# Delta rule: the third inverse level issues all its first steps, two projection triples, then all its second steps, instead of alternating them

## The reference

```
a_mat = jnp.where(strict, jnp.einsum('bhnid,bhnjd->bhnij', kb, k) * decay, 0.0)
ia = a_mat + jnp.eye(c, dtype=a_mat.dtype)
u = lax.linalg.triangular_solve(ia, vb, left_side=True, lower=True, unit_diagonal=True)
w = lax.linalg.triangular_solve(ia, kb * jnp.exp(g)[..., None], left_side=True, lower=True,
                                unit_diagonal=True)
...
def step(s, xs):
    q_c, k_c, u_c, w_c, qk_c, sd_c = xs
    v_new = u_c - jnp.einsum('bhck,bhkv->bhcv', w_c, s)
    o_c = jnp.einsum('bhck,bhkv->bhcv', q_c, s) + jnp.einsum('bhij,bhjv->bhiv', qk_c, v_new)
    s = s * sd_c[..., None, None] + jnp.einsum('bhck,bhcv->bhkv', k_c, v_new)
    return s, o_c
```

## Time and profile before

| | us |
|---|---|
| median of 3 runs | 1801.79 |
| lowest, highest | 1801.58, 1805.0 |
| the profiled execution, its own time | 1799.56 |
| its span | 1797.8 |
| PE busy in the span | 1774.6 |
| DVE busy | 990.5 |
| ACT busy | 720.6 |

### The profile page before, as it was taken

How to read it: one execution, slowest core, us unless ns; L and a number is a source line. 1 busy time by engine, 2 the same in 40 slices (tenths; PEclk the granted TensorE clock), 3 DMA queues, 4 the chain that set the end, 5 groups by cost and what they waited for, 6 DMA issues and landing times.

```text
span 1797.8 us, 26545 instructions
## 1 busy us (share of the span) xinstructions
PE 1774.6 (99%) x10559; PEld 1438.3 (80%) x10559; DVE 990.5 (55%) x1669; ACT 720.6 (40%) x1382; POOL 126.5 (7%) x105
## 2 busy tenths in 40 slices
PE   8999999999999999999999999999999999999999
PEld 6788888888887888888888788468877778888887
DVE  4645656467537444444444755744423688777434
ACT  5644656456345211111134623755223532222324
POOL 1113031221001000000000001520000000000000
PEclk9999999999999999999999999999999999999999
DMA  6422222222324333333223451013313222233221
GB/s 194 85 61 71 61 72 55 56 72 68 109 94 116 107 93 93 98 102 103 94 94 95 91 118 48 24 50 115 118 55 110 71 94 93 93 98 111 95 76 65
DMA packets 183183, 158.18 MB, mean 88 GB/s; under 512 B 36977, under 2 KB 179886, under 8 KB 183050
## 3 DMA queue, kind: packets, MB, share of 16 engines
q1 hardware_dynamic: 172672, 152.88, 27.9%
q0 software_dynamic: 1248, 3.19, 1.3%
q10 hardware_dynamic: 9163, 0.72, 0.4%
HBM read 152.77 MB, written 3.73 MB: 87 GB/s over the span
## 4 chain that ended last, share of the span: by engine, by line
PE 90%; DVE 4%; ACT 3%; issue 1%; DMA 1%; ACTq 0%; POOL 0%; DVEq 0%
PE bank L744 13%; PE bank L746 13%; PE bank L745 13%; PE bank L845 5%; PE bank L847 5%; PE bank L846 5%; PE bank L945 4%; PE bank L734 4%; PE bank L947 4%; PE bank L946 4%; PE bank L1072 1%; PE bank L1083 1%; PE bank L1136 1%; PE bank L1335 1%; PE bank L1094 1%
## 5 line engine op out<-in xcount | busy, mean ns | idle before, releaser
L1539 ACT ACTIVATE w_hi<-ring 128x2048 fp32r<-128x2048 f32 x122 | 234.0, 1918 | 534.2 <-PE bank L746 375.7
L744 PE MATMUL bank<-h_hi,w_hi 128*128 128x512 f32 x1024 | 400.5, 391 | 2.2 <-DVE w_lo L2162 2.0
L746 PE MATMUL bank<-h_hi,w_lo 128*128 128x512 f32 x1024 | 398.5, 389 | 0.0
L745 PE MATMUL bank<-h_lo,w_hi 128*128 128x512 f32 x1024 | 398.4, 389 | 0.0
L2162 DVE TENSOR_TENSOR w_lo<-ring,w_hi 128x2048 fp32r<-128x2048 f32 x108 | 247.3, 2289 | 256.6 <-ACT w_hi L1539 256.6
L744 PEld LDWEIGHTS bank<-h_hi,w_hi 128*128 128x128 f32 x1024 | 192.2, 188 | 44.9 <-issue 3.6
L745 PEld LDWEIGHTS bank<-h_lo,w_hi 128*128 128x128 f32 x1024 | 192.3, 188 | 40.2 <-issue 0.5
L746 PEld LDWEIGHTS bank<-h_hi,w_lo 128*128 128x128 f32 x1024 | 192.3, 188 | 39.8
L845 PE MATMUL bank<-h_hi,w_hi 128*128 128x512 f32 x432 | 170.3, 394 | 1.7 <-DVE arena L2851 1.0
L847 PE MATMUL bank<-h_hi,w_lo 128*128 128x512 f32 x432 | 168.3, 390 | 0.0
L846 PE MATMUL bank<-h_lo,w_hi 128*128 128x512 f32 x432 | 168.1, 389 | 0.0
(11 more groups left out here) (449 smaller groups left out, 2496.5 us busy)
## 6 DMA issues: line engine op xcount, KB each, us to landing
ring<-in_sc_w_in SPq DMA_DIRECT2D x32, 1024.0 KB, 5.4
ring<-in_gdn_w_in SPq DMA_DIRECT2D x24, 1024.0 KB, 5.4
ring<-in_w_up SPq DMA_DIRECT2D x22, 1024.0 KB, 5.1
ring<-in_gdn_w_out SPq DMA_DIRECT2D x8, 1024.0 KB, 5.2
ring<-in_sc_w_out SPq DMA_DIRECT2D x8, 1024.0 KB, 5.2
ring<-in_w_down SPq DMA_DIRECT2D x8, 1024.0 KB, 5.2
ring<-in_w_in SPq DMA_DIRECT2D x4, 1024.0 KB, 5.6
ring<-in_w_mk SPq DMA_DIRECT2D x4, 1024.0 KB, 5.2
```

What stands on the lines that cost most here:

```text
L744: pe.matmul(o, a_hi(k), b_hi(k), start=(k == tiles[0]), stop=False)
L745: pe.matmul(o, a_hi(k), b_lo(k), start=False, stop=False)
L746: mm = pe.matmul(o, a_lo(k), b_hi(k), start=False, stop=(k == tiles[-1]))
L1539: act.activation(w_hi[:, plan[n]["pair"], :], ring[:, n % 2, :], ACT.Copy).then_inc(w_hi_ready, 1)
```

## The change

In the third level (`lv` = 2) the kernel before issues both matmuls of `factor` for one chunk, then both of `update` for one chunk, in turn: `factor` of head 2 with `update` of head 0, `factor` of head 3 with `update` of head 1. The changed kernel has the order of the first two levels there: `factor` of all four heads, two triples, `update` of all four heads. The first two levels keep their order. No instruction is added or taken away, on no engine.

```
-                    factor(0, chunks)
-                    factor(1, chunks)
+                    for h in range(HG):
+                        factor(h, chunks)
+                    next_group(3 if lv == 0 else 2)
+                    for h in range(HG):
+                        update(h, chunks)
                     if lv < 2:
-                        factor(2, chunks)
-                        factor(3, chunks)
-                        next_group(3 if lv == 0 else 2)
-                        update(0, chunks)
-                        update(1, chunks)
-                        update(2, chunks)
-                        update(3, chunks)
                         turn_queries(g, lv)
-                    else:
-                        next_group(2)
-                        for h in range(2):
-                            for t in chunks:
-                                factor(h + 2, [t])
-                                update(h, [t])
-                        update(2, chunks)
-                        update(3, chunks)
                     next_group(2)
```

## The result

Over 20 runs each, the changed kernel has a median of 1804.75 us (1801.72 to 1807.29) and the kernel before 1801.4 us (1798.91 to 1805.0). The ratio is 1.0018, 95% interval 1.0012 to 1.0024: 3.2 us more, between 2.2 and 4.3. That is inside 0.2%, yet clear of zero. The forecast was +2.6 us.

What follows compares the result with a forecast made beforehand. The prediction took PE as the bound, busy 1774.6 of 1797.8 us. Each group gains +0.86 - 0.21 = +0.65 us, four +2.6, so 1801.79 + 2.6 = 1804.4 us, range 1801.0 to 1807.0; chance 0.76.

Steps and rivals of the forecast that it cites:

- The pace: Third level: 64 formerly alternated records pass unmixed at 27.7 ns instead of 14.2, +0.86 us a group.
- The wait that goes: Third level: `update` of head 2 no longer waits for ACT's copy of its product, -0.21 us a group.
- The sum: Third level: +0.86 - 0.21 = +0.65 us a group, +2.6 us over four groups.
- No new wait: Third level and scan: turned matrices 0.5 and 0.7 us early for `factor` of heads 2 and 3; scan not delayed.
- The cover behind the level: Scan's first matmul on `Y_T` comes 4.22 us behind the third level; some 2.4 us in the last group.
- The loss comes through to the end: Whole kernel: PE is the bound, so what its third level takes longer appears in the time, +2.6 us.
- The reason for the pace: Third level's alternated piece: the two steps use different halves of the partitions, so two records pass in one's time.
- The clock: Rival: longer unbroken run of small matmuls, 2.9 us, lowers the clock; 1.7 us once, 6.9 in all groups; chance 0.08.
- Slower loads: Rival, third level: unmixed records held to a weight load's 107 ns, 5.7 us more a group, 1824.6 us; chance 0.01.
- A gain from ACT's earlier copies: Rival: next group's convolution done up to 1.6 us sooner, up to 3.8 us won if PE's scan waited; chance 0.02.
- The median: Whole kernel: median of the runs shown, 1801.79 us, plus 2.6 gives 1804.4 us, 0.14% more.

Runs made afterwards that it cites:

- e6: Kernel before with half the alternation in the third level: only first step of head 3 with second step of head 0; level 4.97 us, ratio 1.0003.
- e2: Kernel before with the third level mixing two heads chunk by chunk within the same step, instead of two steps; level 5.43 us, ratio 1.0017.
- e1: Kernel before with four query transposes moved from the second level's end to behind the third level's alternated piece; level 5.23 us, ratio 1.0002.
- e4: Kernel before with the alternated order in the second level too, query transposes behind the alternated piece; second level 0.13 us shorter, ratio 0.9996.
- e3: Kernel before with the third level alternated by whole heads, 16 records a stretch, instead of chunk by chunk; level 4.84 us, ratio 0.9998.
- e8: Kernel before with the alternated order in the first level too, where both steps use the same tiles; first level up to 2.1 us longer, ratio 1.0033.
- e7: Kernel before with the third level alternated in stretches of two chunks, 8 records of each step; level 4.74 us, ratio 0.9999.
- e5: Changed kernel with one 64x64 weight tile for two of 64x32 in the third level, 64 records for 128; level 5.59 us, ratio 1.0023 to kernel before.

## Why the prediction was right

- **The pace, +0.86 us a group.** Held. All unmixed records pass at 27.7 to 27.9 ns (windows above), e6 gives the same price per record at half the dose, and e2 excludes that the mixing of heads or banks made the difference.
- **The wait that goes, -0.21 us.** Held: no stop for line 1822 is left, and the level is 5.40 us, where 5.61 would stand without the saving. The sum said +0.65 a group, the trace shows +0.67. That the wait was one for the copy rests on e6; e1 doesn't show it.
- **No new wait** at `factor` of heads 2 and 3, at `update` or at the scan: held in all four groups. The cover behind the level is 4.25 us, where 4.2 was forecast. In the last group the prediction had it at 2.4 us, from a pair of triples that included the change to small matmuls; it is 2.2 us in both kernels, which is still enough.
- **The loss comes through to the end.** Held: four levels give 2.7 us, and the measured 3.2 us (2.2 to 4.3) holds it. The 0.5 us between is inside the interval; nothing in the trace calls for a second cause. Part of it may be the draw of the clock. The mean granted clock is 0.9980 over the 20 runs of the changed kernel and 0.9984 over the 35 runs of the kernel before that stand beside e1 to e4. At an equal clock the means differ by 1.9 us (0.997), 2.9 (0.998), 2.4 (0.999) and 2.5 (1.000). Whether the new order itself makes the clock fall more often isn't settled; in e2, whose level is just as long, the mean is 0.9984.
- **The reason for the pace** was right in its first half (different halves of the partitions pass side by side) and too narrow in what I added for e3, that only neighbours in the stream do. In the prediction nothing hung on that.
- **The rivals.** The clock did not fall in any third level of the changed kernel; its windows there say 1.00. The one fall near, inside 112 to 118 us, lies in the first level, behind a wait of 2.31 us, ahead of the changed instructions. For the row that this rival was built on, the reading was loose: the low clock did not come after the 5.2 us of small matmuls but began within them, since the stretch from 1109.00 to 1110.12 alone already has 0.63 in the kernel before. Slower loads are out: the rule of the Trainium skill's page "TensorE: Matmul & The Clock Gate", section "Part 3: Packing small matmuls — row/col tiling", would by the prediction's reading have held each record to 107 ns, and they pass at 27.9. A gain from ACT's earlier copies did not come: ACT is 1.1 us ahead, and nobody waits for it.
- **The median.** 1804.4 was forecast and 1804.75 measured. That it lies so close is in part luck: the forecast started from the median of three runs, 1801.79, which is 0.39 us above that of 20, and this made up for half of what the forecast loss was short (2.6 us against 3.35 between the two medians). The size of the noise was read from those three runs too; in 20 the single runs spread by 6 us, so that 2.7 us shows only in the ratio of many. The spread goes with the clock: among the 35 runs of the kernel before, the 8 at 0.997 have a mean of 1804.2 us, the 4 at 1.000 one of 1799.3.

## What to carry to other kernels

Here, small matmuls that read different partitions and write different ones passed side by side when they stood close in the program (14.2 ns a record against 27.7), so two independent steps of that kind are worth interleaving, in stretches of up to 8 records in this kernel. Before doing it, look whether the two use different tiles: where they shared them the pace stayed (e8), and the unbroken run of 192 tiny records stopped for up to 1.7 us, for a cause that stays open. Put 0.1 to 0.2 us into the sum for each change between small tiles and full ones: here these changes took back all of what filling a wait had won (e1) and most of what a second interleaved level had (e4). And where the profile names a releaser, look when that releaser ended: in e1 it names a copy that was done long before.

## What was not expected of the hardware

PE started matmuls out of the program's order across halves of the partitions: in e3 two records of line 1094 started at 130.78 while six records of line 1083, ahead of them in the program, started between 130.82 and 130.94, and in e7 it was six as well. With stretches of 4 and 8 records the pace is 14.2 and 14.5 ns, with 16 it is 18.8, and unmixed 27.7. Whether the partitions read or those written make the overtaking possible stays open, since the two steps differ in both. That two neighbours differ only in what they write is enough to pass side by side, by e5.
